# Three blocks instead of two take turns in the opening of a two-layer denoising kernel

## The reference

```
shift, scale, gate = split(silu(cond) @ w_ada + b_ada)       # one row per stream
h = rmsnorm(x) * (1 + scale) + shift
layer 0: q, k, v, z = split(h @ w_in, 4)                     # w_in 2048 x 8192
         o = attention (context: full; latent: grid neighbourhood with bias + cached context)
         x = x + gate * ((o * silu(z)) @ w_out)
layer 1: u, z = split(h @ w_in); y = gelu(S5 scan of u, forward and backward)
         y = y * sigmoid(y @ w_glu + b_glu); x = x + gate * ((y * silu(z)) @ w_out)
out = rmsnorm(x) * g
```

## Time and profile before

| | us |
|---|---|
| median of 3 runs | 1120.38 |
| the profiled execution | 1123.26 |
| its span in the trace | 1121.5 |
| TensorE (PE) busy | 1060.8 |
| VectorE (DVE) busy | 767.4 |
| ScalarE (ACT) busy | 541.9 |
| GpSimd (POOL) busy | 232.8 |

### The profile page before, as it was taken

One profiled execution on the slowest core, in us unless ns is written; L12 is line 12 of the kernel. 1 busy time (PEld: TensorE's weight loads), 2 busy tenths in 40 slices (PEclk: granted clock), 3 DMA queues, 4 the chain that ended last, 5 costly groups with the idle time before them and its releaser, 6 DMA issues.

```text
span 1121.5 us, 18581 instructions
## 1 busy us (share of the span) xinstructions
PE 1060.8 (95%) x7426; PEld 827.9 (74%) x7426; DVE 767.4 (68%) x1206; ACT 541.9 (48%) x762; POOL 232.8 (21%) x382
## 2 busy tenths in 40 slices
PE   3888999999999899999999989999999999999996
PEld 2676777777777677778777758888787877878885
DVE  2663765767676565767688866459998997576665
ACT  5323535343443344445544356566667466355442
POOL 1010420343034311332233340200222232100000
PEclk8999999999999999999999989999998999999999
DMA  9999987999799987976599986877573868674552
GB/s 378 419 419 420 361 326 267 340 354 355 281 339 378 359 316 285 351 263 231 227 386 352 350 302 249 274 252 233 193 261 131 271 212 310 224 303 157 188 195 102
DMA packets 62406, 325.61 MB, mean 290 GB/s; under 512 B 8208, under 2 KB 14992, under 8 KB 30192
## 3 DMA queue, kind: packets, MB, share of 16 engines
q1 hardware_dynamic: 42944, 267.93, 64.1%
q0 software_dynamic: 12176, 45.33, 11.6%
q10 hardware_dynamic: 7200, 11.16, 2.8%
HBM read 296.04 MB, written 28.34 MB: 289 GB/s over the span
## 4 chain that ended last, share of the span: by engine, by line
PE 72%; DMA 11%; DVE 10%; ACT 4%; issue 2%; SPq 0%; ACTq 0%; POOL 0%; DVEq 0%
PE ps L828 19%; PE ps L830 18%; PE ps L829 18%; DMA araw<-in_wada 5%; PE ps L702 5%; DMA early<-in_wada 4%; DVE wlo L1495 3%; PE ps L938 2%; DVE sb L1607 2%; ACT whi L1099 2%; DMA araw<-in_wadag 2%; DVE t L1604 1%; PE ps L771 1%; PE ps L962 1%; PE ps L754 1%
## 5 line engine op out<-in xcount | busy, mean ns | idle before, releaser
L1495 DVE TENSOR_TENSOR wlo<-raw,whi 128x1024 fp32r<-128x1024 f32 x284 | 347.2, 1226 | 229.7 <-ACT whi L1099 225.5
L1099 ACT ACTIVATE whi<-raw 128x1024 fp32r<-128x1024 f32 x284 | 298.9, 1058 | 408.8 <-PE ps L830 395.1
L828 PE MATMUL ps<-whi,xhi 128*128 128x512 f32 x1136 | 461.8, 407 | 8.3 <-DVE wlo L1495 5.1
L829 PE MATMUL ps<-wlo,xhi 128*128 128x512 f32 x1152 | 451.9, 392 | 0.0
L830 PE MATMUL ps<-whi,xlo 128*128 128x512 f32 x1136 | 445.8, 392 | 0.0
L828 PEld LDWEIGHTS ps<-whi,xhi 128*128 128x128 f32 x1136 | 215.2, 189 | 83.2 <-issue 19.2
L830 PEld LDWEIGHTS ps<-whi,xlo 128*128 128x128 f32 x1136 | 214.5, 189 | 47.4
L829 PEld LDWEIGHTS ps<-wlo,xhi 128*128 128x128 f32 x1152 | 218.2, 189 | 41.0
L702 PE MATMUL ps<-araw,cT 128*32 128x512 f32 x512 | 62.5, 603 | 3.1 <-DMA araw<-in_wadag 3.0
L1619 DVE TENSOR_TENSOR sb<-sb,t 128x128 f32<-128x128 f32 x140 | 49.4, 356 | 4.6
L524 POOL COPY bbf<-bb 64x256 f32<-64x256 f32 x16 | 17.1, 1066 | 107.6 <-DVE bb L1415 98.8
(11 more groups left out here) (233 smaller groups left out, 1089.6 us busy)
## 6 DMA issues: line engine op xcount, KB each, us to landing
raw<-in_w SPq DMA_DIRECT2D x144, 1024.0 KB, 6.4
araw<-in_wadag SPq DMA_DIRECT2D x64, 1024.0 KB, 8.8
early<-in_wada SPq DMA_DIRECT2D x20, 1024.0 KB, 18.0
araw<-in_wada SPq DMA_DIRECT2D x12, 1024.0 KB, 17.8
ctab_scratch<-ce POOLq DMA_DIRECT2D x16, 512.0 KB, 8.4
btab_scratch<-bs ACTq DMA_DIRECT2D x32, 256.0 KB, 6.3
btab<-btab_scratch SPq DMA_DIRECT2D x16, 512.0 KB, 4.2
ctab<-ctab_scratch POOLq DMA_DIRECT2D x16, 512.0 KB, 4.9
```

The source lines that it names most:

```text
L828: mm(acc, xhi[:, kt, st], hi[:, k], start=kt == 0, stop=False)
L829: mm(acc, xhi[:, kt, st], wlo[:, slot, k0 % 2, k], start=False, stop=False)
L1099: af(whi_at(k).rearrange("p k c -> p (k c)"), src, ACT.Copy).then_inc(s_hi, 1)
L1495: tt(wlo[:, slot, k % 2].rearrange("p k c -> p (k c)"), src, whi_at(k).rearrange("p k c -> p (k c)").bitcast(F32), ALU.subtract).then_inc( ...
```

## The change

`T_IN0` becomes 3. Blocks 0, 1 and 2 (q, k, v of head group 0) take turns by unit for the first 24 units; units 3c, 3c+1 and 3c+2 use eighth c. Pairs 2, 3, 4, 5, ... stand ahead of units 0, 1, 3, 4, ..., eighth c is finished ahead of unit 3c-2, and the last pair, 15, stands ahead of unit 19. The order of the loads follows (`pairs_at`): loads 0 to 9 of `w` stand ahead of the last pair, where it was 0 to 7. Block 2 accumulates in banks 6 and 7; so `early_columns` goes to bank 4 beside the sums, with a wait for VectorE's reading of it ahead of the next eighth, and the tables of quarters 0 and 1 go to bank 5, where the transposed x goes too, with waits between the two. The splits of the opening are made one or two units ahead; the lead of four is built up in units 21 to 28. `attention_inputs(0)` waits for unit 19 in place of unit 13. Attention of head group 0 starts at unit 24 and ends at unit 34 (before: 17 and 31); the other head groups keep their units. The remaining modulation is in blocks 3 to 14 and 16 to 19, and is taken out at blocks 7, 11, 15 and 20, one unit later in the block.

```
-T_IN0 = 2
+T_IN0 = 3
 def table_units(n):
     if n < 3:
-        return ((3, 8, 6, 10, 10), (11, 15, 15, 19, 20), (17, 21, 20, 27, 28))[n]
+        return ((3, 8, 7, 14, 14), (11, 17, 18, 23, 23), (21, 29, 25, 30, 31))[n]
+def transposed_at(n):
+    return ((8, 11), (17, 20))[n] if n < 2 else (table_units(n)[1], table_units(n)[1] + 1)
 def ada_beside(b):
-    return 2 <= b < 14 or B_OUT0 <= b < B_OUT0 + 4
+    return T_IN0 <= b < 15 or B_OUT0 <= b < B_OUT0 + 4
-FIN_B = (6, 10, 14, B_IN1)
+FIN_B = (7, 11, 15, B_IN1)
+def pair_unit(p):
+    return -1 if p < 2 else T_IN0 * ((p - 2) // 2) + (p - 2) % 2
+def eighth_at(k):
+    return k // T_IN0 + 1 if k < T_IN0 * (EARLY - 1) and k % T_IN0 == 1 else None
 def pairs_at(g):
-    if g < 2:
-        return ((0, 1), (2,))[g]
-    return tuple(p for p in (2 * g - 1, 2 * g) if p < N_EARLY // 2)
+    return tuple(p for p in range(N_EARLY // 2) if (g == 0 or 2 * g - 3.2 <= pair_unit(p) - 0.25) and pair_unit(p) - 0.25 < 2 * g - 1.2)
 def table_bank(n, half):
-    return 6 if n == 0 else 5 + half
+    return 5 if n < 2 else 5 + half
+ATTENTION = ("q", "k", "scores", "softmax", "exp", "sums", "pT", "pv", "div", "gated")
+ATT_0 = (24, 25, 26, 27, 28, 29, 32, 33, 33, 34)
+ATT_HB = (11, 19, 23, 24, 25, 26, 29, 30, 30, 31)
 def splits_at(k):
-    if k in (14, 15):
-        return (2 * k - 12, 2 * k - 11)
+    if k < 29:
+        return {21: (22,), 22: (23, 24), 23: (25,), 24: (26, 27), 25: (28,), 26: (29, 30), 27: (31,), 28: (32,)}.get(k, ())
 def acc_bank(b):
-    return 4 if b == B_TURNS + 2 else 2 * ((b + (b > B_TURNS + 2)) % 2)
+    if b < T_IN0:
+        return (0, 2, 6)[b]
+    return 4 if b == B_TURNS + 2 else 2 * ((b + 1 + (b > B_TURNS + 2)) % 2)
...
 GpSimd
-                    pool.wait_ge(s_wused, 14)
+                    pool.wait_ge(s_wused, 20)
                     attention_inputs(hb)
...
 TensorE
+                        pe.wait_ge(s_adaEout, c)                       # ada_early, first load of eighth c
-                tr(ps[:, 7, c % 4 * P:(c % 4 + 1) * P], adasb[:, c % 2, 0:P], ident[:]).then_inc(s_adaE, 1)
+                tr(ps[:, 4, (1 + c % 2) * P:(2 + c % 2) * P], adasb[:, c % 2, 0:P], ident[:]).then_inc(s_adaE, 1)
+                            if n < 2:                                  # tables: transposes
+                                pe.wait_ge(s_xlo, (k + 2) // T_IN0 + 1)
+                if i == 0 and g in (4, 5, 7):                          # transposed x
+                    pe.wait_ge(s_bs, {4: 1, 5: 2, 7: 3}[g])
+                if i == 0 and g == 6:
+                    pe.wait_ge(s_bandd, 1)
+                if n == 2:                                             # tables: transposes of quarter 2
+                    pe.wait_ge(s_sub, 3)
-                if k < 2 * EARLY - 2:
-                    ada_early(k + 2)
-                    if k % 2 == 1:
-                        transposed(0, (k + 1) // 2)
-                        early_columns((k + 1) // 2)
+                for p in range(2, N_EARLY // 2):
+                    if k == pair_unit(p):
+                        ada_early(p)
+                if eighth_at(k):
+                    transposed(0, eighth_at(k))
+                    early_columns(eighth_at(k))
...
 ScalarE (VectorE likewise, with its own parts of each step)
-                if k < 2 * EARLY - 2 and k % 2 == 1:
-                    c = (k + 1) // 2
-                    adasb_early(c)
+                if k < T_IN0 * (EARLY - 1) and k % T_IN0 == 0:
                     split(k + 1)
-                    high(0, c)
+                if eighth_at(k):
+                    adasb_early(eighth_at(k))
+                    split(k + 1)
+                    high(0, eighth_at(k))
                     split(k + 2)
```

More of the change, by code:

```diff
@@ L191, in tiles_gone, with attention_at @@
     return TG * i + same[-1] + 1 if same else 0
[L194 to L200, removed]
+ATTENTION = ("q", "k", "scores", "softmax", "exp", "sums", "pT", "pv", "div", "gated")
+ATT_0 = (24, 25, 26, 27, 28, 29, 32, 33, 33, 34)
+ATT_HB = (11, 19, 23, 24, 25, 26, 29, 30, 30, 31)
+def attention_at(k, what):
+    i = ATTENTION.index(what)
+    return next((hb for hb in range(4) if k == (32 * hb + ATT_HB[i] if hb else ATT_0[i])), None)
 def splits_at(k):
     last = UB * (B_END - 1)
-    if k in (14, 15):
-        return (2 * k - 12, 2 * k - 11)
+    if k < 29:
+        return {21: (22,), 22: (23, 24), 23: (25,), 24: (26, 27), 25: (28,), 26: (29, 30), 27: (31,), 28: (32,)}.get(k, ())
     if k < last - 2:
@@ L466, in _ @@
                         load_u(w)
[L467 to L470, removed]
                 b, half = (g // NCK - 1, 1) if g % NCK == 1 else (g // NCK, 0)
-                if g % 2 == 1 and (b, half) > (2, 0) and ada_beside(b):
+                if g % 2 == 1 and ada_beside(b):
                     for c in (2 * half, 2 * half + 1):
@@ L476, in _ @@
                             sp.wait_ge(s_ada1, n - 1)
+                        else:
+                            sp.wait_ge(s_ada0, N_EARLY - 1 + n)
                         sp.dma_start(araw[:, n % 2], d["wadag"][n // KT, :, n % KT]).then_inc(s_araw[n % 2], 16)
@@ L747, in tables @@
                                     pe.wait_ge(s_bandd, n)
-                            if n == 0 and half == 1:
-                                pe.wait_ge(s_bs, 1)
+                            if n < 2:
+                                pe.wait_ge(s_xlo, (k + 2) // T_IN0 + 1)
+                                if half == 1:
+                                    pe.wait_ge(s_bs, 2 * n + 1)
                             for r in range(2):
@@ L811, in unit @@
                     pe.wait_ge(s_xlo, TG * STAGES.index(B_TURNS) + AHEAD)
-                elif u == 0 and b >= 2:
-                    wait_evacuated(pe, b - 3 if b in (B_TURNS + 3, B_TURNS + 4) else b - 2)
+                elif u == 0 and b >= T_IN0:
+                    wait_evacuated(pe, b - 3 if b in (T_IN0, T_IN0 + 1, B_TURNS + 3, B_TURNS + 4) else b - 2)
                 pe.wait_ge(s_lo, k0 + 1)
@@ L846, in q_or_k, with attention @@
                 last.then_inc(s, 1)
-            def attention(hb, b, u):
-                j = b % 4
-                if (j, u) == q_at(hb):
+            def attention(k, b):
+                hb = attention_at(k, "q")
+                if hb is not None:
                     wait_evacuated(pe, 4 * hb)
-                    pe.wait_ge(s_bandd, 3 * hb + 1)
+                    pe.wait_ge(s_bandd, 3 * hb + 1 if hb else 2)
                     pe.wait_ge(s_bs, 2 * (3 * hb + 1) if hb else 4)
@@ L855, in attention @@
                         pe.wait_ge(s_og, 2 * hb)
-                    q_or_k(qkvz[:, 0], 5, s_qT)
-                if (j, u) == k_at(hb):
+                    else:
+                        pe.wait_ge(s_adaEout, EARLY)
+                    q_or_k(qkvz[:, 0], 5 if hb else 4, s_qT)
+                hb = attention_at(k, "k")
+                if hb is not None:
                     wait_evacuated(pe, 4 * hb + 1)
@@ L862, in attention @@
                         pe.wait_ge(s_bs, 2 * (3 * hb + 2))
+                    else:
+                        wait_evacuated(pe, T_IN0 - 1)
                     q_or_k(qkvz[:, 1], 5, s_kT)
-                if (j, u) == (2, 7):
+                hb = attention_at(k, "scores")
+                if hb is not None:
                     pe.wait_ge(s_kTsb, 2 * (hb + 1))
-                    pe.wait_ge(s_bs, 2 * (3 * hb + 3))
+                    if hb >= 1:
+                        pe.wait_ge(s_bs, 2 * (3 * hb + 3))
                     pe.wait_ge(s_attin, 48 * (hb + 1))
-                    pe.wait_ge(s_adaout, fins(b))
+                    if fins(b):
+                        pe.wait_ge(s_adaout, fins(b))
                     for h in range(HB):
@@ L874, in attention @@
                     last.then_inc(s_sc, 1)
-                if (j, u) == (3, 5):
+                hb = attention_at(k, "pT")
+                if hb is not None:
                     pe.wait_ge(s_prob, 3 * (hb + 1))
                     pe.wait_ge(s_bandd, 3 * hb + 3)
+                    pe.wait_ge(s_bs, 2 * (3 * hb + 3))
                     for i in range(3):
-                        if i == 2:
+                        if i == 2 and hb >= 1:
                             pe.wait_ge(s_adaout, fins(b))
@@ L884, in attention @@
                     last.then_inc(s_pT, 1)
-                if (j, u) == (3, 6):
+                hb = attention_at(k, "pv")
+                if hb is not None:
                     wait_evacuated(pe, 4 * hb + 2)
@@ L1062, in tables @@
                     for half in range(2):
-                        if k == units[1] + half:
+                        if k == transposed_at(n)[half]:
                             if n >= 1:
@@ L1144, in attention @@
                     for st in range(NS):
-                        af(qT[:, st], ps[:, 5 + st], ACT.Copy, scale=QSCALE).then_inc(s_qTsb, 1)
-                if (j, u) == k_at(hb):
```

(23 more changed lines are left out.)

54 lines of the change are left out of this document (26 added, 28 removed).

## The result

| | before | after |
|---|---|---|
| median of the runs, us | 1120.27 (1115.71 to 1120.52, 5 runs) | 1109.83 (1109.23 to 1113.45, 5 runs) |
| ratio, with its 95% interval | | 0.9918 (0.9895 to 0.9940) |
| profiled execution / its span, us | 1123.26 / 1121.5 | 1111.23 / 1109.4 |

The kernel became faster by 10.4 us; 7.7 were forecast, with 1112.7 as the time. On two more chips the changed kernel came to 0.9906 (0.9892 to 0.9921) and 0.9909 (0.9888 to 0.9930) of the kernel before. The measured 1109.83 lies 1.2 us under the band around the forecast (1111 to 1115) and inside the whole range (1108.5 to 1118.0).

A forecast was written before the change was run, and what follows sets the result against it. Transfers were taken to bound the opening to some 117 us, TensorE the rest. 17.3 + 0.8 - 5.6 - 3.8 - 1.0 = 7.7 us faster, so 1112.7 us; band 1111 to 1115, whole range 1108.5 to 1118.0.

The forecast's parts named there:

- Bound by transfers: Opening, 0 to some 117 us: DMA transfers set the pace, TensorE the rest; some 19 us of waiting open to work.
- Item 1: Ahead of the last pair: two more loads of w and a btab_scratch store, last pair let go at 121.9; cost 5.6 us.
- Item 2: By the last pair: six more units (13 to 18) and transposes of a table half already done; gain 17.3 us.
- Item 3: Unit 14's wait for xlo of eighth 7 goes, a unit more lying before its first user; gain 0.8 us.
- Item 4: Hand-over after the last pair: short split lead makes units 20 to 23 wait, 2.6 at unit 23 behind b_bar(2); cost 3.8 us.
- the even eighths' 0.5: Opening, even eighths: VectorE does modulated ahead of a split, which ends some 0.5 us after the unit before it.
- Item 5: After the hand-over: softmax wait at unit 29 (0.4) and modulation taken out at blocks 11 and 15 (0.6); cost 1.0 us.
- the wait of 3.0 for one of them stays: Later w_ada tiles move by one block; PE's 3.0 us wait for one of them was taken as unchanged.
- A: PE and its helpers bound the opening, 0.8 us lost per eighth over six, 4.8 less gain, 1117.5 us; chance 0.18.
- C: Slower: late units hold back free slots, DMA runs dry every eighth; at 2 us each 4.3 slower, 1124.7; chance 0.07.
- D: Gain given back: later waits absorb it or the third block doesn't fill waits, within 2 us of before; chance 0.07.
- B: Smoother hand-over: GpSimd done early, unit 23 waits 0.5, units 20 to 22 none; 3.3 us more, 1109.4; chance 0.20.

The follow-up runs named there:

- e5: Kernel before, each of the 32 early modulation loads bringing only half (512 KB), read twice by the matmuls; 1097.39 us, 0.9809 of before.
- e6: Changed kernel, each early modulation load bringing only half (512 KB), read twice by the matmuls; 1106.83 us, 0.9887 of before.
- e4: Changed kernel with GpSimd's attention inputs of head group 0 moved behind its quarter 1; 1107.80 us, 0.9903 of before.
- e9: Changed kernel run a third time, no edit; 1109.47 us, 0.9909 of before.
- e1: Changed kernel run again beside the kernel before, no edit; 1108.32 us.
- e7: Kernel before with only the transposed modulation columns moved to bank 4 and the wait of each next eighth; 1.0001 of before.
- e11: Changed kernel with gate load late, attention inputs behind quarter 1, splits 22 to 24 a step earlier, split ahead of modulated; 1104.25 us, 0.9868 of before.

## Why the prediction was right, point by point

*Bound by transfers (right).* The old opening loses 21 us when half of the early loads goes (e5), the new one some 3 (e6).

*Item 1, 5.6 us for more loads ahead of the last pair (right in size, not at the end).* The last pair started at 120.74 without waiting; its last load landed at 121.4, where 121.9 was forecast, and at 116.2 in the kernel before: 5.2 us later. Load 10 of `w`, next in the queue, is what ScalarE's split of unit 20 waited for until 124.31, against 124.5 in the working. By transfers the last pair is where it was put; PE met it with about nothing to spare.

*Item 2, 17.3 us of work done by then (right).* Units 13 to 18 and the half table are done at 120.7. A rule of the Trainium skill was weighed there: "TensorE: Matmul & The Clock Gate" (Part 1) says activity releases the throttle. The window 58.8 to 73.0 went from 0.88 to 1.00 of the granted clock, as by that rule. Whether it brought a gain of its own wasn't tried; DMA stayed at its full share there, which speaks against it. The other page of the Trainium skill weighed there, "DMA: Bandwidth & Descriptors" (Specifications), works out its 358 GB/s as half of what a stack gives two cores. Here one core ran, and the trace has 419 GB/s over 90.7 us, so that figure didn't bound it.

*Item 3 (right).* No wait for `xlo` is left up to 160 us.

*Item 4, 3.8 us at the hand-over (right in cause, the size partly luck).* 0.53 at unit 20, 0.85 at unit 22, 2.25 at unit 23, 3.6 in sum; unit 23 at 139.08 (139.1 forecast). The cause was named rightly, and e4 showed it. To a tenth of a us the agreement is luck: the same kernel in e9 waited 0.62, 0.94 and 1.03, 2.6 in sum. The way over `par` also adds up to 135.3 in the working's own terms (126.5 + 4.4 - 1.1 + 5.5), not to 136. What released `b_bar(2)` was `par`; GpSimd's `ce` was done 0.9 earlier. Waits in the opening that I had set to nothing beyond the even eighths' 0.5, 1.61 us at unit 5, where the powers and `b_bar(0)` stand on VectorE, and 0.30, 0.58 and 0.30 later, didn't hold up the last pair: it started without waiting, before its last load had landed.

*Item 5, later costs 1.0 (right in sum, not in its parts).* There is no wait for softmax at unit 29 (0.4 forecast). Blocks 11 and 15 cost 1.2 us in place of 0.6.

*Sum.* Forecast for the part up to block 9: 17.3 + 0.8 - 5.6 - 3.8 - 0.4 = 8.3; the unit starts give 8.5, and 8.6 and 9.6 in the traces of e1 and e9.

*The step that failed* is "the wait of 3.0 for one of them stays". It fell to 0.77, and the low clock after it went too: 4.5 us in the profiled executions. The wait isn't the change's doing: it is absent in e7, with the old order, and in e1 and e9, with the new. In the medians the gain beyond the forecast is 2 to 3.5 us; moving the gate load gave the kernel before 1.3, which is the most that this wait can account for there, and the rest is within the scatter. A late load beside another engine's large transfer is no fixed cost; I should have bounded it by 0 and 4.5.

*The rivals.* A and C are excluded by the 8.5 us in the opening; D by the ratio; B's time (1109.4) is nearer the measured one than the forecast's, but not by its mechanism: units 20 to 23 waited as in the forecast (unit 23 less in e9). e11 is what B described.

## What to carry to other kernels

Where a stretch is bounded by transfers, move in work that needs few of them per microsecond of the idle engine, and stop when the two are level; past that point it costs, as e6 shows. Where several engines follow written orders, the lead of the helpers has to be kept at the hand-over: here a wait on GpSimd that had been free with a lead of four units cost 1.0 to 2.3 us with a lead of one, and moving three lines gave it back. Compare two traces by the start of every unit, not by the spans: the lead came at two places with different causes, and only one of them was the change's. And take more than one trace of a kernel before a wait of a few us is put down to a change: the one at block 9 was there in one trace of the old order and not in the other.

## What was not expected of the hardware

A short wait can cost more by the clock than by itself, and not in every run. In block 26 PE waits 1.85 us in 835 to 845 us in both of these traces. After it, the changed kernel's granted clock was 0.66 over the next 10 us, e4's was 1.00, and over units 208 to 214 the changed kernel lost 3.15 us against e4. In e9 it was 0.83, and 1.6 us. The windows of the changed kernel, then of e4:
```profile
835.00:845.00 10.00, 8.15 (x70) 6.58 (x69) 9.42 (x20) 9.78 (x16) 2.63 (x4) 1.00 0.31 112
845.00:855.00 10.00, 10.00 (x102) 8.19 (x99) 8.21 (x18) 6.85 (x10) 0.57 (x1) 0.66 0.15 63
```
```profile
835.00:845.00 10.00, 8.15 (x82) 6.79 (x81) 9.42 (x20) 9.81 (x15) 2.63 (x4) 1.00 0.34 108
845.00:855.00 10.00, 10.00 (x147) 8.36 (x147) 7.87 (x20) 8.95 (x13) 0.57 (x1) 1.00 0.21 60
```
Over all 13 traces units 208 to 214 took one of three times: 35.4 us in five (the kernels before and changed among them, so the main comparison isn't touched), 33.8 in four and 32.2 in four (e4, e7 and e11 among them). That such places make part of the 4 to 5 us by which single runs scatter is argued, not shown.
